# A hybrid gMLP and band-attention layer: head pairs in cycles of two instead of single steps

## What is computed

```python
h = x @ w_in                                  # u_a, v_a, z_a, q, k, v_b, z_b
a_out = gelu(u_a) * (tril(w_s) @ layernorm(gelu(v_a)) + b_s)
# B: chunks of 64 frames, a query sees its own chunk and the 8 before it
scores = q @ k.T * 64 ** -0.5 + bias[head, relative position]
o = softmax(where(valid, scores, -inf)) @ v
y = concat(a_out * silu(z_a), o * silu(z_b))
out = layernorm(2 ** 0.25 * x + y @ w_out)
```

## Time and profile before

| | us |
|---|---|
| median of 3 runs | 1091.03 |
| the profiled execution's own time | 1090.57 |
| its span | 1088.5 |
| TensorE busy | 1065.5 (98%) |
| VectorE busy | 465.5 (43%) |
| ScalarE busy | 327.7 (30%) |
| GpSimd busy | 213.3 (20%) |

### The profile page before, as it was taken

One profiled execution on the slowest core, in us unless ns is written; L12 is line 12 of the kernel. 1 busy time (PEld: TensorE's weight loads), 2 busy tenths in 40 slices (PEclk: granted clock), 3 DMA queues, 4 the chain that ended last, 5 costly groups with the idle time before them and its releaser, 6 DMA issues.

```text
span 1088.5 us, 17631 instructions
## 1 busy us (share of the span) xinstructions
PE 1065.5 (98%) x7320; PEld 909.0 (84%) x7320; DVE 465.5 (43%) x964; ACT 327.7 (30%) x636; POOL 213.3 (20%) x163
## 2 busy tenths in 40 slices
PE   7999999999999999999999999999999999999997
PEld 5988889999999999999999877777777777788875
DVE  6635442212112111121112014677667767777755
ACT  6410011111111111121112134454544444555430
POOL 0111112020110000000000000553444333444331
PEclk9999999999999999999999999999999999999999
DMA  9571113221221333333331444785555444444422
GB/s 340 184 189 39 49 39 120 79 86 62 73 64 54 116 115 129 116 123 112 119 107 64 126 154 138 213 285 165 149 148 167 123 149 141 136 139 144 126 88 79
DMA packets 129966, 137.33 MB, mean 126 GB/s; under 512 B 7496, under 2 KB 103904, under 8 KB 129888
## 3 DMA queue, kind: packets, MB, share of 16 engines
q1 hardware_dynamic: 124992, 121.54, 35.6%
q10 hardware_dynamic: 4896, 14.68, 4.1%
HBM read 86.62 MB, written 52.72 MB: 128 GB/s over the span
## 4 chain that ended last, share of the span: by engine, by line
PE 92%; DMA 2%; DVE 2%; POOL 1%; ACT 1%; issue 1%; POOLq 0%; DVEq 0%; SPq 0%; ACTq 0%
PE s_ps L1168 34%; PE s_ps L1185 16%; PE out_ps L1341 15%; PE pt_ps L1168 8%; PE o_ps L1318 6%; PE s_ps L1246 5%; PE pt_ps L1280 4%; PE s_ps L1341 2%; DMA big_raw<-w_all 1%; DVE prob L1056 1%; POOL wo_l L717 1%; PE o_ps L1197 1%; PE out_ps L1197 1%; DMA bias<-s_skew 1%; PE s_ps L1208 1%
## 5 line engine op out<-in xcount | busy, mean ns | idle before, releaser
L1168 PE MATMUL s_ps<-xh,ring 128*128 128x512 f32 (+1 forms) x1200 | 341.4, 362 | 0.8 <-ACT st L841 0.8
L1168 PEld LDWEIGHTS s_ps<-xh,ring 128*128 128x128 f32 x1200 | 221.3, 188 | 24.5 <-issue 1.2
L1168 PE MATMUL s_ps<-xl,ring 128*128 128x512 f32 (+1 forms) x600 | 217.2, 362 | 0.0
L1185 PE MATMUL s_ps<-ring,xh 128*128 128x512 f32 x544 | 171.0, 396 | 0.0
L870 ACT ACTIVATE pt<-pt_ps 128x1024 f32<-128x1024 f32 (+3 forms) x112 | 78.9, 704 | 166.9 <-PE pt_ps L1280 166.7
L1168 PEld LDWEIGHTS s_ps<-xl,ring 128*128 128x128 f32 x600 | 112.7, 188 | 11.8
L1185 PEld LDWEIGHTS s_ps<-ring,xh 128*128 128x128 f32 x544 | 99.8, 188 | 20.2
L1185 PE MATMUL s_ps<-ring,xl 128*128 128x512 f32 x272 | 106.0, 390 | 0.0
L1037 DVE CUSTOM_DVE_ANT_1 prob<-s_ps,bias 128x640 f32<-128x640 f32 (+1 forms) x112 | 85.6, 801 | 45.3 <-PE s_ps L1246 45.3
L1341 PE MATMUL out_ps<-wo_h,yh 128*128 128x512 f32 x248 | 103.0, 415 | 0.5 <-POOL wo_l L717 0.5
L877 ACT ACTIVATE prob<-prob,low 128x640 f32<-128x640 f32 (+3 forms) x136 | 100.2, 740 | 5.2 <-DVE low L1037 5.0
(11 more groups left out here) (132 smaller groups left out, 1227.7 us busy)
## 6 DMA issues: line engine op xcount, KB each, us to landing
raw<-w_all ACTq DMA_DIRECT2D x26, 512.0 KB, 3.6
yr<-s_y SPq DMA_DIRECT2D x17, 512.0 KB, 5.0
r<-x SPq DMA_DIRECT2D x17, 512.0 KB, 3.6
q<-s_q SPq DMA_DIRECT2D x16, 512.0 KB, 4.2
k<-s_k SPq DMA_DIRECT2D x16, 512.0 KB, 5.5
y_out<-r SPq DMA_DIRECT2D x15, 512.0 KB, 4.0
s_y<-st SPq DMA_DIRECT2D x24, 256.0 KB, 2.3
x_raw<-x_t SPq DMA_DIRECT2D x12, 384.0 KB, 12.8
```

Of the source, the lines that this page charges most:

```text
L1168: last = nc.tensor.matmul(bank[b][:, 0:width], w[:, kc, :], xx[:, kc, :], start=kc == 0 and a == 0, stop=kc == KC - 1 and a == 2)
L1185: last = nc.tensor.matmul(out, xx[:, kc, cols], ring[:, 0:GRP, side, kc, :], start=kc == 0 and a == 0, stop=kc == KC - 1 and a == 2)
```

## The change

The loop over steps becomes a loop over 42 cycles of two units. TensorE's order within a cycle c is: the fifth block of unit 2c-3, scores of 2c, turn of 2c-2, sums of 2c-3, then 24 matmuls in one go (a whole v tile, or half an output tile), the fifth block of 2c-2, scores of 2c+1, turn of 2c-1, sums of 2c-2. So an odd unit's sums come a cycle later than those of the even unit before it. The other queues are rewritten to that order. There are six slots of prob instead of four. z moves to where yr was, and yr lies where yl lies, so that the low part is written over y in place; the load of y then waits for the outputs of the tile two before (`out_done`) instead of for the split (`y_split`). The stream tile becomes output tile 12 instead of 15. Of the residual part, the sum and the statistics become two functions with the odd unit's biases between them.

```diff
-V_STEPS = 2 * (TILES - V_EARLY)
-STEPS = V_STEPS + 4 * TILES
-ORDER = [*range(PTILES - 1), PTILES, PTILES - 1]
+V_CYCLES = TILES - V_EARLY
+CYCLES = V_CYCLES + 2 * TILES
+ORDER = [*range(12), PTILES, *range(12, PTILES)]
+START = [V_CYCLES + 2 * n for n in range(TILES)]
+def gate_cycle(unit):
+    return (unit + 4) // 2
+LATE = [n for n in range(TILES) if GATED[ORDER[n]] >= START[n] - 1]
+SLOTS = 6
...
+        yr = [at(f"yr{s}", x_at[3 + s] + 20480, [KC, P]) for s in range(2)]
...
 # SP, load_y
-                    sp.wait_ge(y_split, n - 1)
+                    sp.wait_ge(out_done, 2 * n - 2)
...
 # SP, in the loop
+                if 1 <= cycle <= V_CYCLES:
+                    store_v(V_EARLY + cycle - 1)
-                if step == V_STEPS:
+                if cycle == V_CYCLES:
                     sp.wait_ge(proj_done, DONE["v", TILES - 1])
                     for j in range(4, 8):
                         load_wo(j)
...
 # ScalarE
+            for cycle in range(CYCLES):
+                if is_stream(2 * cycle - 4):
+                    keep_sums(2 * cycle - 4)
+                copy_fifth(2 * cycle - 3)
+                for n in LATE:
+                    if START[n] == cycle:
+                        y_high_part(n)
+                exponents(2 * cycle - 1)
+                copy_first(2 * cycle - 2)
+                exponents(2 * cycle)
+                if is_stream(2 * cycle - 3):
+                    keep_sums(2 * cycle - 3)
+                for n in range(TILES):
+                    if START[n] - 1 == cycle and n not in LATE:
+                        y_high_part(n)
+                copy_fifth(2 * cycle - 2)
+                copy_first(2 * cycle - 1)
+                if cycle < V_CYCLES:
+                    copy_v(V_EARLY + cycle)
...
 # VectorE
+            for cycle in range(CYCLES):
+                if closes_tile(2 * cycle - 4):
+                    gate(UNITS[2 * cycle - 4][1])
+                if is_stream(2 * cycle - 4):
+                    gate_stream(UNITS[2 * cycle - 4][1])
+                for n in LATE:
+                    if START[n] == cycle:
+                        y_low_part(n)
+                biases(2 * cycle)
+                if closes_tile(2 * cycle - 3):
+                    gate(UNITS[2 * cycle - 3][1])
+                normalise_all(2 * cycle - 1)
+                normalise_all(2 * cycle)
+                for n in range(TILES):
+                    if START[n] - 1 == cycle and n not in LATE:
+                        y_low_part(n)
+                for unit in (2 * cycle + 2, 2 * cycle + 3):
+                    if is_stream(unit):
+                        place_stream(UNITS[unit][1])
+                n, h = divmod(cycle - V_CYCLES, 2)
+                if n >= 0:
                     residual(n, h)
+                if is_stream(2 * cycle - 3):
+                    gate_stream(UNITS[2 * cycle - 3][1])
+                biases(2 * cycle + 1)
+                if n >= 0:
+                    statistics(n, h)
                     if h == 1:
                         moments(n)
...
 # TensorE
+            def middle(cycle):
+                if cycle < V_CYCLES:
+                    project_tile("v", V_EARLY + cycle, 0, KC)
                 else:
+                    n, h = divmod(cycle - V_CYCLES, 2)
+                    for c0 in range(0, KC, 4):
+                        project_out(n, h, c0, c0 + 4)
+            for cycle in range(CYCLES):
+                turn_fifth(2 * cycle - 3)
+                score(2 * cycle)
+                if is_stream(2 * cycle - 4):
+                    turn_back(UNITS[2 * cycle - 4][1])
+                turn_first(2 * cycle - 2)
+                weigh_unit(2 * cycle - 3)
+                middle(cycle)
+                if is_stream(2 * cycle - 3):
+                    turn_back(UNITS[2 * cycle - 3][1])
+                turn_fifth(2 * cycle - 2)
+                score(2 * cycle + 1)
+                turn_first(2 * cycle - 1)
+                weigh_unit(2 * cycle - 2)
```

More of the change, by code:

```diff
@@ L584, in _ @@
                     load_v(1)
[L586 to L605, removed]
+            for cycle in range(CYCLES + 2):
+                for unit in (2 * cycle, 2 * cycle + 1):
+                    if opens_tile(unit):
+                        sp.wait_ge(scored, HEADS_BEFORE[unit])
+                        load_qk(UNITS[unit][1] + 1)
+                if cycle == 2:
+                    sp.wait_ge(proj_done, DONE["v", 10])
+                    load_z(0)
+                    load_z(1)
+                for unit in (2 * cycle - 4, 2 * cycle - 3):
+                    if opens_tile(unit + 1):
+                        t = UNITS[unit + 1][1]
+                        sp.wait_ge(weighed, unit + 1)
+                        if t == 1:
+                            sp.wait_ge(mix_done, TILES)
+                        if t == 3:
+                            sp.wait_ge(ya_full, GRP * NCH)
+                            sp.wait_ge(kf_stored, 16 * GRP)
+                        load_v(t + 1)
+                        sp.wait_ge(gated, t)
+                        load_z(t + 1)
+                if 1 <= cycle <= V_CYCLES:
+                    store_v(V_EARLY + cycle - 1)
                 for t in range(PTILES):
-                    if GATED[t] == step:
+                    if GATED[t] == cycle:
                         sp.wait_ge(gated, t + 1)
@@ new lines, in copy_first, with copy_fifth, exponents @@
+            def copy_first(unit):
+                if 0 <= unit < NU:
+                    for e in range(2 if is_stream(unit) else 1):
+                        copy_turned(unit, e)
+            def copy_fifth(unit):
+                if 0 <= unit < NU and not is_stream(unit) and turned_copies(unit) > 1:
+                    copy_turned(unit, 1)
+            def exponents(unit):
+                if 0 <= unit < NU:
+                    for h in range(heads_of(unit)):
+                        exponent(unit, h)
@@ new lines, in score, with turn_first, turn_fifth, weigh_unit @@
+            def score(unit):
+                if is_stream(unit):
+                    stream_scores(unit)
+                elif unit < NU:
+                    scores(unit)
+            def turn_first(unit):
+                if 0 <= unit < NU:
+                    turn(unit, 0)
+            def turn_fifth(unit):
+                if 0 <= unit < NU and not is_stream(unit) and turned_copies(unit) > 1:
+                    turn(unit, 1)
+            def weigh_unit(unit):
+                if 0 <= unit < NU:
+                    weigh(unit)
```

140 lines of the change are left out of this document (48 added, 92 removed).

## The result

The changed kernel takes 1105.59 us (median of 5 runs, 1102.97 to 1107.23), where the one before takes 1091.03: 1.3% slower, ratio of the runs 1.0131, 95% interval 1.0117 to 1.0145. Forecast were 1080.1 us and a range of 1072 to 1088. The prediction was wrong in its sign.

What follows compares the result with a forecast made beforehand. Bound by TensorE's own queue plus its waits. Terms -18.4 + 0.5 + 4.5 + 4.0 + 0.3 + 3.7 + 2 - 7.5 = -10.9 took the median of 1091.03 to 1080.1 us, 1.0% faster; range 1072 to 1088.

Steps and rivals of the forecast that it cites:

- the port's 2: VectorE's scalings held by GpSimd's product or addition: one cycle with two held ones, +2 us, bounds 0 and 30.
- the streams' 4.0: Stream units' shorter sums and turning uncover ScalarE's copy or the bias, four times each: +4.0 us.
- the 2.8 of stream scores that were to go: TensorE's 2.8 us of waits ahead of stream scores, expected to vanish with operands placed half a cycle ahead.
- Part 4: TensorE's waits for stream scores, late normalisation and others go, -7.5 us; VectorE held up by GpSimd instead, +2.
- rival 2: GpSimd's two 2.4 us operations catch two scalings in most tiles, odd biases come late: 1112 us, slower; chance 0.10.
- point of decision: Held scalings matter if the even unit's first scaling starts after 6.0 in the cycle; expected start 4.5 to 5.2.
- Part 2: Less TensorE work covers the softmax chains: +0.5 us in full cycles, +4.5 where runs are short, +4.0 streams, +0.3 late y tile.
- Part 1: Fewer changes of matmul shape on TensorE: about 0.6 us gained per full cycle, -18.4 us together, bounds -7 and -19.
- rival 1: Surplus belongs to waiting instructions, not shapes; fifth block to scores costs 0.2 too: 1091.3 us, no change; chance 0.13.
- Waits that go: TensorE's waits, 5.0 us by the table and 7.5 estimated with outputs and drain, go: -7.5 us, bounds -3 and -8.
- Part 3: 24 outputs in one go need the split weights sooner: wait 3.7 us against 0.5, bounds 0.5 and 5, no clock fall.
- The short cover of the v stage: Early tiles' short runs don't cover the bias, and unit 16's scores wait 0.75 for the v copy: +4.5 us.

Runs made afterwards that it cites:

- the first experiment: The changed kernel with the three small copies that place a stream's queries and keys moved from VectorE to ScalarE; 1091.64 us, ratio to the kernel before 1.0006.

## Why the prediction was wrong

The kernels without product and addition and those without streams part the 14.6 us into three, and the prediction's terms can be put beside them:

| part | measured | forecast |
|---|---|---|
| pairs alone, no port (1067.70 - 1072.56) | -4.9 | -11.7 |
| stream units (23.3 in the new order, 14.1 in the old) | +9.2 | -1.2 |
| GpSimd's product and addition (14.6 and 4.4) | +10.2 | +2 |
| sum | +14.6 | -10.9 |

The forecast of the first row is the sum less the port's 2, the streams' 4.0, the 2.8 of stream scores that were to go, and four of the 28 cycles (2.4), which the 8 streams fill. The misses are 6.8, 10.4 and 8.2. Any one of them alone would have left a gain of 0.5 us or more; it took two to turn the sign. The 2.8 stands in the row of the streams because the prediction wrote it there; as shown below, 2.1 of it was made by the product and the addition. Moved to the third row, it leaves that one a forecast of -0.1 and a miss of 10.3, and the streams a miss of 8.3.

**The port (Part 4) is the single term of the sum that failed most, 10.2 where 2 stood.** (The streams' row takes in three terms.) Its mechanism was named, and the row read rightly: a held VectorE instruction ends with GpSimd's. The step that failed is the count of what is held: it was made over scalings alone. By my own order VectorE ends the even unit's scalings at 6.0 behind the fifth block and GpSimd's product starts at 6.0. What VectorE does from there on is place the next stream's operands, three copies whose code stands in the diff, and I had counted them only as "placed half a cycle ahead, so these go". At four of the eight streams they fall under the product and the addition: two held copies (2.37 and 2.31 us) at two of them, and at the other two a copy of 2.36 behind a scaling of 2.50. Held scalings alone, on which rival 2 was built, are absorbed: in the kernel after one of them takes up to 2.68, as it does in the first experiment, which has 14 us less. In that experiment the scaling that answers to 817.34 takes its 2.50 us as well (from 814.77), and the bias is still in time. Twice even two held scalings in a row (843.47 and 846.26, 966.90 and 969.68) cost TensorE no more than the 0.25 and 0.16 us that it waits there in the first experiment too. So rival 2 had the right engine and the wrong instructions, and its point of decision (a scaling starting after 6.0) wasn't the deciding one; its 1112 lay nearer than the forecast, but not for its reason. The Trainium skill's rule on the port pair ("SBUF — State Buffer", "Who interferes with whom"), by which the loser is blocked for a whole instruction of the other engine, held in these rows as in the halves: 2.4 us for a whole instruction, 1.2 for half of one.

**The stream units (Part 2) cost 9.2 net and save nothing.** I priced the lost cover at 4.0 and took 2.8 off for the stream scores that no longer wait. The first experiment's turnings wait 14 times, 4.9 us, for ScalarE's copy, and the new order without streams has

```profile
PE s_ps L1298 <- DVE low L1067: 4.8, 8, 1.3
PE out_ps L1393 <- POOL wo_l L730: 3.4, 1, 3.4
PE pt_ps L1332 <- ACT pt L881: 1.2, 2, 0.6
```

so that 12 waits, 3.7 us, come with the streams, four for the gate, 0.8, and four of 0.16 to 0.25 for a bias, 0.7: 5.2, where 4.0 stood. The waits that were to go were mostly the port's: without product and addition the old order has only

```profile
PE s_ps L1256 <- issue: 0.7, 1, 0.7
```

of its 2.8 left. The rest of the 9.2, 4.7 (9.2 - 5.2 + 0.7), is in no wait of the tables. The miss of 10.4 is then 1.2 of waits, 2.1 of waits that were the port's, 2.4 of gain that the cycles with a stream were to have, and these 4.7. I take them for runs of other shapes that follow one another. TensorE in the first experiment, around a stream unit:

```profile
793.52 0.34 PE L1336 MATMUL pt_ps<-ident,prob 64*128 64x64 f32 x4
793.67 1.23 PE L1302 MATMUL s_ps<-k,q 64*128 64x512 f32 x12
...
796.66 0.34 PE L1336 MATMUL pt_ps<-ident,prob 64*128 64x64 f32 x4
796.93 0.45 PE L1314 MATMUL s_ps<-kt,qd 128*32 128x144 f32 x8
```

The fifth block takes 0.27 ahead of stream scores and 0.15 ahead of a pair's. The 4.7 is a difference of four kernels and as uncertain as they are (1 to 2 us); that it lies in such places is argued and not shown row by row.

**Fewer changes of shape (Part 1) gave 0.41 a cycle, not 0.60.** The period was forecast at 11.4 to 11.5 and is 11.64. In the cycle above the scores straight behind the fifth block take 0.98 and 0.97 to the next run, as much as the 1.00 behind outputs nearly: the entry that I costed at nothing for a 64-row neighbour is paid. That is a part of rival 1, and 0.17 of the 0.21 by which the cycle is over 12.05 - 0.62 = 11.43. The second sums take 1.24 and the first 1.31; the 0.07 I take for a wait for ScalarE's copy (it ends at 997.35, and the fifth block starts at 997.49), whose margin I gave as 0.07. The two fifth blocks take 0.08 less than costed, the rest 0.05 more. 24 cycles by 0.19 are 4.6 of the 6.8 us missed in the pairs.

**Waits that go.** Of the 7.5, 2.5 was an estimate beyond the table. Among pairs alone, without product and addition, the old order waits 1.9 us for prob, 0.8 for the residual (r) and 0.5 for the weights, and the new order has none of the first two, so 3.2 went where 4.7 stood: 1.5 more. The 2.5 has no run behind it: what the tables hold beyond the 5.0 of the earlier trace rows is the 0.9 for r and the 0.5 for the weights.

**The weights (Part 3).** The wait was forecast as 3.7 and is 3.1 to 3.5; that it would come without a fall of the clock was wrong. The granted clock of the earlier trace rows at 1.00 behind the last matmul was no witness for a wait in mid-kernel: here the granted clock is 0.62 behind 3.07 us of waiting, at 1.1 to 1.6 us. What the Trainium skill says in "TensorE: Matmul & The Clock Gate", Part 1, that a TensorE left idle is throttled, was the better guide; the trace agrees with it in kind, and the 1.9 us that the prediction worked out for that case is near the 1.6. With the 4.6 and the 1.5 above this fall makes 7.2 to 7.7 for the pairs, and the short cover below about 1 more: 1.5 to 2 over the 6.8, which I leave unresolved. The port's three falls are 5.0 of its price.

**What was right.** The short cover of the v stage within about 1 us (8 waits for a bias, 4.8 us, and 0.7 for the v copy, where 4.5 stood for both), one long wait in cycle 9, and scores that don't wait in a full cycle of pairs. The chances were too sure: 0.10 for the port, though the prediction's own times put GpSimd's start and VectorE's end on the same 6.0.

## What to carry to other kernels

When work is moved to another place of an engine's order, list every small instruction that lands there and lay it beside what GpSimd does at that time: in this kernel a copy of 0.19 us that started under GpSimd's product or addition lasted until that one ended (scalings did too), and what it delays is what is queued behind it. Here it paid to put the small copies on ScalarE, or to cut the GpSimd operations in pieces. Before the loads of something late are issued sooner, look at what the work behind the first landing takes: here that was 14.2 us of GpSimd's time, and no earlier issue shortened it. A wait of 2 to 3 us is priced with its clock: in this kernel 9.0 us of waits brought 5.0 us of slower matmuls with them.

## What the runs showed of the hardware

- Holds come one GpSimd instruction at a time. Between product and addition (794.34 to 794.41) VectorE got through with a copy of 0.18 us, and the next was held again.
- A wait of 2.03 us (824.70) stood ahead of 6.8 us at the lower clock, one of 2.29 us (798.19) of none: behind it the granted clock is still 1.00:

```profile
799.00:811.00 12.00, 11.79 (x136) 9.51 (x133) 6.90 (x18) 5.67 (x11) 0.00 (x0) 1.00 0.55 157
```

  With the product and the addition in halves, waits of 0.88 and 0.87 us (820.05 and 938.66), each with one of 0.53 just before, are followed by it too: the granted clock is 0.58 from 820 to 824 and 0.64 from 940 to 944. The length of a wait alone doesn't tell which comes.
- An earlier issue of 2 MB of loads landed nothing sooner at a DMA share of 1.07 (first piece at GpSimd at 718.32 and 718.14 for 717.03). SP stood 8 to 10 us at the wait for the store issued behind them, so that vc and yr were loaded 6.5 to 8.6 us later.
